# Four GEMM results in flight in PSUM in place of two, each in one bank

## The chip, the cores and the metric

The kernel runs on one core of one Trainium2 chip. The metric is the device time of one execution in microseconds. Three runs of the kernel before took 2454.41, 2458.18 and 2463.07 us (median 2458.18).

## The reference, cut to what matters

The input is x of [1, 256, 1024] in fp32, and everything is computed in fp32. One `first_block` is followed by two layers of `second_block`. Cut down to its products and what stands between them:

```
first_block:  mod = silu(c) @ w_mod + b_mod
              z = adaLN(x) @ w_in ; windowed attention, gated recurrence, blockwise attention
              x += gate * ((g0*p_a + g1*p_b + g2*p_c) @ w_out)
              x += gate * (silu(u_gate) * u_val) @ w_down      # u = causal conv over h @ w_up
second_block, twice:
              x += 0.5 * norm(swiglu(norm(x)))
              u = norm(x) @ w_in -> u_conv, q, k, v, u_pool, gates
              y_conv = silu(layer_norm(depthwise conv31(a*sigmoid(g)))) @ conv_pw
              y_attn = diff_attention(q, k, v) @ attn_o        # 8 heads of two score maps
              y_pool = ((windowed mean of u_pool - u_pool) @ w_grp * scale) @ pool_o
              x += norm((g0*y_conv + g1*y_attn + g2*y_pool) @ w_out)
              x += norm(cross_attention(norm(x), norm(mem)))
              x += 0.5 * norm(swiglu(norm(x)))
```

In `pool_branch` the 1024 columns of u_pool form four groups of 256. Each group gets its own moving mean over 2, 4, 8 or 16 rows, and its own 256x256 product `w_grp`.

## The kernel before, in words

Tokens: 256. Every dense product is a sequence of **units**: 512 KB of weights, which are four 128-row slices of 256 columns. A **GEMM result** (a "pair" in the code, numbered from 0 by `gemm`, L100) is two tiles of 128 x 256, accumulated over all units of its input features: 8 slices of features make two units. A GEMM in form F keeps features on the partitions (L866), in form T tokens (L869). fp32 precision comes from three matmuls per slice and tile: a high part of the weights with a high part of x, the same with the low part of x, and the low part of the weights with the high part of x. So a unit of four slices and two tiles is 24 matmuls.

Engines and queues of a unit m: SP starts the weights' transfer into one of 6 raw buffers as soon as that is free; ACT rounds them to the high part (`hi`, L1142) once the unit m-4 has left its buffer; DVE subtracts to get the low part (`lo`, L1475), three units ahead of PE; PE multiplies (`pe_unit`, L846 to L872). TensorE, DVE and ACT each run one instruction list in one common order of steps, which `plan()` writes out before the program is built. `spread` (L147) lays short pieces of other work behind the units: softmaxes of the attention, the taps of the depthwise convolution (L1925), windows of the pool branch. An engine that waits holds up everything behind it in its own list.

The results of GEMMs lie in `gemm_ps` (L638), four banks of PSUM, as [2 results][2 tiles][512 columns]. A tile of 256 columns fills half of a bank, so each of the two tiles of a result has a bank of its own. The other four banks (`misc_ps`) take scores, turned tiles and statistics. Before the first matmul of result p, PE waits until result p-2 has been read out (L852). Each tile's first matmul has the start flag and its last one the stop flag (L863, L864). A result is read by one or two engines (an evacuation, queued on the reader's list behind the `hi` or `lo` of the unit just before it): for the query features `vec_scaled` on DVE (L1666), for the pool inputs and values `vec_v2` on DVE (L1673, one instruction per tile), for the pool products first ACT (`act_evac_pool_w`, L1444, one per tile: the high part) and then DVE (`vec_pool_w`, L1943, one per tile: the rest).

The stretch that matters below lies in each layer of the second block, in `queries_pool` (about L455 to L485). Its steps are: pool inputs 2 and 3 (columns 512 to 1023), query features 1, window 3, pool inputs 0 and 1, window 2, query 2, window 1, query 3, window 0, and then the four pool products g = 3, 2, 1, 0. The eight heads of the differential attention are spread between them; per head PE makes scores (L1016, and L1017 for the bias), DVE takes the row maximum (L1685), ACT the exponential (L1273), DVE normalises (L1721), PE turns the result (L1034), and DVE and ACT copy it for the product with v (L1054, L1055).

Before the change the pool inputs are a GEMM of 512 columns: one result then fills its two banks, with 128x512 matmuls at L869, in four units of two slices each.

Of the kernel before, what the change touches and what calls it, by code (L numbers as in the profile page):

```python
# [17 lines left out]
F32 = mybir.dt.float32  # L18
# [5 lines left out]
P = 128  # L24
T = 256
# [15 lines left out]
RAW = 6  # L41
SPLIT = 4
AHEAD = SPLIT - 1
CONV_PARTS = 10
CONV_TAPS = (CONV_K - 1) // CONV_PARTS
NEG = -1e30
# [39 lines left out]
def plan(stop=None):  # L86
# [348 lines left out]
    def mixer(l):  # L435
# [18 lines left out]
        def queries_pool():  # L454

            after = readers.get("G")

            def inputs(j):
                z2(l, "pool", j, "evac_v2", form="T", cols=2 * COLS, dst="pt", c0=j * COLS)

            def query(j):
                z2(l, "q", j, "evac_scaled", dst="q", ft=2 * j, by=HD ** -0.5)

            def window(g):
                add("window", l=l, g=g, gen=key + "p", after=after, s=new_stat())

            inputs(2)
            query(1)
            window(3)
            inputs(0)  # L470
            window(2)
            query(2)
            window(1)
            query(3)
            window(0)
            for g in (3, 2, 1, 0):
                gemm("pool_w", 0, 2, ("G", key + "p"), "evac_pool_w", ft0=2 * g, l=l, g=g)
            merge(0, 8, "pool_o", "q", True)
# [97 lines left out]
def build(nc, a, out, scratch, marks, final, stop=None):  # L576
# [55 lines left out]
    MGS = {"b1": SQ[:], "m": o_m["pu"][:]}  # L632
    last_x = max([k["v"] for kind, k in steps if kind == "residual"], default=0)
    n_pairs = 1 + max([k["id"] for kind, k in steps if kind.startswith("evac")], default=-1)
    last_pairs = [p for p in (n_pairs - 2, n_pairs - 1) if p >= 0]


    GP = ctx.enter_context(nc.psum_tensor("gemm_ps", [P, 2, 2, 512], F32))  # L638
    PB = ctx.enter_context(nc.psum_tensor("misc_ps", [P, 4, 512], F32))
    GPF = GP[:].rearrange("p a b c -> p (a b c)")  # L640
    PBF = PB[:].rearrange("p a b -> p (a b)")
# [55 lines left out]
        return ap.unsqueeze(1).to_broadcast([P, n, T])  # L697

    def slot(pid):
        return GP[:, pid % 2, :, 0:T]  # L700

    def unit_of(buf, i, u):

# [135 lines left out]
    def _(pe):  # L839
# [6 lines left out]
        def pe_unit(u):  # L846
            xh, xl = xbuf(*u["x"])
            m = u["m"] % SPLIT
            pe.wait_ge(sems["weights_rest"], at("rest", u["m"]))
            if u["first"]:  # L850
                if u["pair"] >= 2:
                    pe.wait_ge(*done(("evac", u["pair"] - 2)))  # L852
                else:
                    pe.wait_ge(sems["vec_setup"], at("x", 0, 3))
            ps = GP[:, u["pair"] % 2, :, :]
            tiles = u["cols"] // P if u["form"] == "F" else TT
            for kt in range(u["nkt"]):
                for c in range(tiles):
                    f = u["ft0"] + u["kt0"] + kt
                    if c == 0:  # L860
                        pe.wait_ge(*done(("split", *u["x"], f)))
                    for n, (w, x) in enumerate(((WH, xh), (WH, xl), (WL, xh))):
                        start = u["first"] and kt == 0 and n == 0  # L863
                        stop_ = u["last"] and kt == u["nkt"] - 1 and n == 2  # L864
                        if u["form"] == "F":
                            mm = pe.matmul(ps[:, c, 0:T], w[:, m, kt, c * P:(c + 1) * P], x[:, f, :],  # L866
                                           start=start, stop=stop_)
                        else:
                            mm = pe.matmul(ps[:, c, 0:u["cols"]], x[:, f, c * P:(c + 1) * P],  # L869
                                           unit_of(w, m, u)[:, kt, :], start=start, stop=stop_)  # L870
            mm.then_inc(sems["gemm_done"], 1)
            up("gemm_done", ("unit", u["n"]))  # L872
# [260 lines left out]
    def _(act):  # L1133
# [125 lines left out]

        def act_evac_v1(k):  # L1260
            act.wait_ge(sems["gemm_done"], at("unit", k["last_unit"]))
            act.copy(BUF[k["dst"]][:, :, k["c0"]:k["c0"] + k["cols"]], GP[:, k["id"] % 2, :, 0:k["cols"]]).then_inc(sems["act_drain"], 1)
            up("act_drain", ("evac", k["id"]))
            mark(("tm", k["dst"], 0), "act_drain")

# [203 lines left out]
    def _(dve):  # L1469
# [200 lines left out]
        def vec_v2(k):  # L1670
            dve.wait_ge(sems["gemm_done"], at("unit", k["last_unit"]))
            for t in range(TT):
                dve.tensor_scalar(BUF[k["dst"]][:, t, k["c0"]:k["c0"] + k["cols"]], GP[:, k["id"] % 2, t, 0:k["cols"]], RT[:, t:t + 1], None, ALU.mult).then_inc(sems["vec_drain"], 1)  # L1673
                up("vec_drain", ("evac", k["id"]))
            mark(("tm", k["dst"], k["l"]), "vec_drain")
            for c in range(k["c0"], k["c0"] + k["cols"], COLS):
                mark(("tm", k["dst"], k["l"], c), "vec_drain")
# [259 lines left out]
        def vec_pool_w(k):  # L1937
            l, g = k["l"], k["g"]
            dve.wait_ge(sems["gemm_done"], at("unit", k["last_unit"]))
            for i in range(2):  # L1940
                f = 2 * g + i
                dve.wait_ge(sems["act_split"], at("split_hi", "G", f"l{l}mq", f))
                dve.scalar_tensor_tensor(out=o_m["gl2"][:, f, :], in0=slot(k["id"])[:, i, :], scalar=col(f"pscale{l}", f), in1=o_m["gh2"][:, f, :], op0=ALU.mult, op1=ALU.subtract).then_inc(sems["vec_split"], 1)  # L1943
                up("vec_split", ("split", "G", f"l{l}mq", f))
            mark(("evac", k["id"]), "vec_split")
# [171 lines left out]
```

## Time and profile before

| | |
|---|---|
| three runs | 2454.41, 2458.18, 2463.07 us |
| profiled execution | 2459.62 us, span 2457.8 us |
| granted TensorE clock, mean | 0.967 of full speed |
| TensorE (PE) | 2329.1 us busy, 95%, 17913 matmuls |
| weight loads (PEld) | 2225.7 us, 91% |
| VectorE (DVE) | 1697.4 us, 69% |
| ScalarE (ACT) | 1201.9 us, 49% |
| GpSimd (POOL) | 87.8 us, 4% |
| DMA | 397 MB read, 162 GB/s over the span |
| chain that ended last | PE 77%, DVE 15%, ACT 5%, issue 3% |

How to read it: an engine that is busy for 95% of the span is nearly always the one that the others wait for, so what a change can win is to be looked for in the stretches in which PE stands still, and in those in which its clock is granted at half speed. "issue" as a releaser means that the profile shows nothing that ended the wait; a wait for a semaphore that another engine raised can also end up under it. A row of the timeline gives start, busy time, engine and line, tiles (out<-in), and in brackets the idle time before it and what ended it. Matmuls overlap, so the distance between two starts is the cost of one, not its own length.

### The profile page before, as it was taken

The page shows a single profiled execution, that of the slowest core. Times are in us where ns is not written, and L with a number is a line of the kernel's source. Part 1 is how long each engine was busy: PE and PEld are TensorE (multiplying, and loading weights), DVE is VectorE, ACT ScalarE, POOL GpSimd, SP SyncE. Part 2 cuts the span into 40 slices and gives each one's busy share as a digit, 9 for nine tenths or more (in the row PEclk, how much of TensorE's full clock was granted, in tenths as well). Part 3 has the DMA queues.
Part 4 walks back from the last instruction along what each step waited for, and adds up shares of the span by engine and source line. Part 5 has one row for each costly group of instructions (what it writes and reads, how often), then busy time and mean ns, then how long its engine had stood idle before and what let it go on. Part 6 is the DMA issues. An engine that isn't in the chain of part 4 may idle for free.

```text
span 2457.8 us, 43525 instructions
## 1 busy us (share of the span) xinstructions
PE 2329.1 (95%) x17913; PEld 2225.7 (91%) x17913; DVE 1697.4 (69%) x2655; ACT 1201.9 (49%) x1803; POOL 87.8 (4%) x78
## 2 busy tenths in 40 slices
PE   6998898999999999999999999999999999999997
PEld 5977898999999987889898999999997889898997
DVE  6656887986664897787555664664897787555653
ACT  2565446764444434555535444444434555535443
POOL 1000000110110000000000110110000000000110
PEclk7998999999999999999999999999999999999998
DMA  8634575667656563346444655656553346444662
GB/s 241 189 103 145 161 251 160 200 188 225 182 176 190 172 179 95 112 129 189 145 139 137 181 182 159 182 176 188 173 180 95 112 130 188 146 139 136 183 184 81
DMA packets 397941, 400.89 MB, mean 163 GB/s; under 512 B 18006, under 2 KB 391112, under 8 KB 397745
## 3 DMA queue, kind: packets, MB, share of 16 engines
q1 hardware_dynamic: 395361, 389.27, 52.1%
q0 software_dynamic: 2384, 8.85, 1.1%
q8 instruction: 143, 2.34, 0.4%
q14 instruction: 53, 0.43, 0.1%
HBM read 396.98 MB, written 1.09 MB: 162 GB/s over the span
## 4 chain that ended last, share of the span: by engine, by line
PE 77%; DVE 15%; ACT 5%; issue 3%; DMA 1%; DVEq 0%; ACTq 0%; POOL 0%; POOLq 0%
PE gemm_ps L866 62%; DVE weights_lo L1475 4%; PE gemm_ps L869 4%; DVE y L1925 3%; PE misc_ps L1017 2%; PE misc_ps L1016 2%; PE misc_ps L951 2%; PE misc_ps L969 1%; DVE mod_partial L1572 1%; ACT weights_hi L1142 1%; ACT e L1273 1%; DVE y L1625 1%; PE misc_ps L1049 1%; PE misc_ps L1034 1%; PE misc_ps L1013 1%
## 5 line engine op out<-in xcount | busy, mean ns | idle before, releaser
L1475 DVE TENSOR_TENSOR weights_lo<-raw_weights,weights_hi 128x1024 fp32r<-128x1024 f32 x704 | 836.5, 1198 | 448.3 <-ACT weights_hi L1142 446.4
L866 PE MATMUL gemm_ps<-h_hi,weights_hi 128*128 128x256 f32 x3536 | 1008.8, 285 | 41.8 <-DVE h_lo L1611 27.6
L1142 ACT CAST weights_hi<-raw_weights 128x1024 fp32r<-128x1024 f32 x704 | 719.0, 1034 | 673.1 <-PE gemm_ps L866 609.5
L866 PE MATMUL gemm_ps<-h_lo,weights_hi 128*128 128x256 f32 x3536 | 995.5, 282 | 0.0
L866 PE MATMUL gemm_ps<-h_hi,weights_lo 128*128 128x256 f32 x3536 | 994.1, 281 | 0.0
L866 PEld LDWEIGHTS gemm_ps<-h_hi,weights_hi 128*128 128x128 f32 x3536 | 673.5, 190 | 50.4 <-issue 46.3
L866 PEld LDWEIGHTS gemm_ps<-h_lo,weights_hi 128*128 128x128 f32 x3536 | 673.1, 190 | 2.9 <-issue 2.2
L866 PEld LDWEIGHTS gemm_ps<-h_hi,weights_lo 128*128 128x128 f32 x3536 | 671.2, 190 | 0.0
L866 PE MATMUL gemm_ps<-hidh,weights_hi 128*128 128x256 f32 x880 | 248.4, 282 | 1.8 <-DVE weights_lo L1475 1.8
L866 PE MATMUL gemm_ps<-hidl,weights_hi 128*128 128x256 f32 x880 | 246.6, 280 | 0.0
L866 PE MATMUL gemm_ps<-hidh,weights_lo 128*128 128x256 f32 x880 | 246.3, 280 | 0.0
L1925 DVE SCALAR_TENSOR_TENSOR y<-zp,param_cols,y 128x256 f32<-128x256 f32 x480 | 196.6, 477 | 0.0
L866 PE MATMUL gemm_ps<-gh,weights_hi 128*128 128x256 f32 x544 | 163.8, 301 | 11.6 <-issue 9.3
L866 PEld LDWEIGHTS gemm_ps<-hidh,weights_hi 128*128 128x128 f32 x880 | 166.0, 189 | 2.2 <-DVE weights_lo L1475 2.0
L866 PEld LDWEIGHTS gemm_ps<-hidh,weights_lo 128*128 128x128 f32 x880 | 165.9, 188 | 0.0
L866 PEld LDWEIGHTS gemm_ps<-hidl,weights_hi 128*128 128x128 f32 x880 | 165.7, 188 | 0.2
L866 PE MATMUL gemm_ps<-gl,weights_hi 128*128 128x256 f32 x544 | 157.2, 289 | 0.0
L866 PE MATMUL gemm_ps<-gh,weights_lo 128*128 128x256 f32 x544 | 157.2, 289 | 0.0
L866 PEld LDWEIGHTS gemm_ps<-gh,weights_hi 128*128 128x128 f32 x544 | 107.9, 198 | 15.0 <-issue 12.8
L2043 POOL TENSOR_TENSOR hidl<-hf,hidh 128x512 fp32r<-128x512 f32 x55 | 73.4, 1335 | 1241.5 <-ACT hidh L1398 1241.5
L866 PEld LDWEIGHTS gemm_ps<-gl,weights_hi 128*128 128x128 f32 x544 | 107.8, 198 | 1.4 <-issue 1.0
L866 PEld LDWEIGHTS gemm_ps<-gh,weights_lo 128*128 128x128 f32 x544 | 107.6, 198 | 0.0
(289 smaller groups left out, 2665.9 us busy)
## 6 DMA issues: line engine op xcount, KB each, us to landing
raw_weights<-in_ffn_w_dram SPq DMA_DIRECT2D x256, 512.0 KB, 3.9
raw_weights<-in_w_in_dram SPq DMA_DIRECT2D x200, 512.0 KB, 3.7
raw_weights<-in_w_mod_dram SPq DMA_DIRECT2D x48, 512.0 KB, 4.9
raw_weights<-in_w_up_dram SPq DMA_DIRECT2D x44, 512.0 KB, 4.6
raw_weights<-in_xattn_kv_dram SPq DMA_DIRECT2D x32, 512.0 KB, 4.4
raw_weights<-in_w_out_dram SPq DMA_DIRECT2D x24, 512.0 KB, 4.5
raw_weights<-in_w_down_dram SPq DMA_DIRECT2D x20, 512.0 KB, 4.5
raw_weights<-in_w_branch_dram SPq DMA_DIRECT2D x16, 512.0 KB, 4.6
```

The costliest lines, as they stand in the source:

```text
L866: mm = pe.matmul(ps[:, c, 0:T], w[:, m, kt, c * P:(c + 1) * P], x[:, f, :], start=start, stop=stop_)
L869: mm = pe.matmul(ps[:, c, 0:u["cols"]], x[:, f, c * P:(c + 1) * P], unit_of(w, m, u)[:, kt, :], start=start, stop=stop_)
L951: mm = pe.matmul(STAT[:, 0:T], ONES[:], squares[:, f, :], start=f == 0, stop=f == NF - 1)
L969: mm = pe.matmul(STAT[:, 0:T], ONES[:], SQ[:, f, :], start=f == 0, stop=f == NF - 1)
L1013: mm = pe.matmul(ps, c["q"][0][f][:, qt * P:(qt + 1) * P], c["k"][0][f], start=f == 0, stop=f == 1)
L1016: pe.matmul(ps, c["q"][m][:, qt * P:(qt + 1) * P], c["k"][m][:, 0:nk], start=True, stop=False)
L1017: mm = pe.matmul(ps, FLIP[:], c["hank"][:, c["head"][m], T - nk:T], start=False, stop=True)
L1034: mm = pe.transpose(TURN[:, at_:at_ + P], c["E"][:, qt, m, kb * P:(kb + 1) * P], IDENT[:])
L1142: act.copy(unit_of(WH, m % SPLIT, u), unit_of(RAWB, u["raw"] % RAW, u)).then_inc(sems["weights_rounded"], 1)
L1475: dve.tensor_tensor(unit_of(WL, m % SPLIT, u), unit_of(RAWB, u["raw"] % RAW, u), unit_of(WH, m % SPLIT, u), ALU.subtract).then_inc(sems["w ...
L1925: dve.scalar_tensor_tensor(out=Y[:, f, :], in0=o_m["zp"][:, f, j:j + T], scalar=col(f"dw{l}", 8 * j + f), in1=Y[:, f, :], op0=ALU.mult, op ...
L2043: pool.tensor_tensor(l_[:, s, :], src, h[:, s, :], ALU.subtract).then_inc(sems["hidden_rest"], 1)
```

## The change

Three things, in the kernel's own names.

1. `gemm_ps` becomes [4 results][2 tiles][256 columns]. It is the same four banks, but both tiles of a result now lie in one bank. PE waits for result p-4 instead of p-2, and the end of the kernel waits for the last four evacuations instead of the last two.
2. The start flag stands only at the first matmul of a result's first tile, and the stop flag only at the last matmul of its last tile. One start clears the written-flags of the whole bank; the first matmul of the second tile then finds its elements unwritten and overwrites them.
3. A result can't be wider than 256 columns per tile any more. So each GEMM of 512 columns for the pool inputs is now two of 256 (`for c in (j, j + 1)`), each of two units of four slices, with two evacuations `evac_v2`, the first of which is queued two units earlier. And in `vec_pool_w` DVE waits before its first read until ACT has read both tiles, because they share a bank.

```diff
+RING = 4
...
             def inputs(j):
-                z2(l, "pool", j, "evac_v2", form="T", cols=2 * COLS, dst="pt", c0=j * COLS)
+                for c in (j, j + 1):
+                    z2(l, "pool", c, "evac_v2", form="T", dst="pt", c0=c * COLS)
...
-    last_pairs = [p for p in (n_pairs - 2, n_pairs - 1) if p >= 0]
-    GP = ctx.enter_context(nc.psum_tensor("gemm_ps", [P, 2, 2, 512], F32))
+    last_pairs = range(n_pairs - RING, n_pairs)
+    GP = ctx.enter_context(nc.psum_tensor("gemm_ps", [P, RING, 2, COLS], F32))
...
     def slot(pid):
-        return GP[:, pid % 2, :, 0:T]
+        return GP[:, pid % RING]
...
             if u["first"]:
-                if u["pair"] >= 2:
-                    pe.wait_ge(*done(("evac", u["pair"] - 2)))
+                if u["pair"] >= RING:
+                    pe.wait_ge(*done(("evac", u["pair"] - RING)))
...
-            ps = GP[:, u["pair"] % 2, :, :]
+            ps = slot(u["pair"])
...
-                        start = u["first"] and kt == 0 and n == 0
-                        stop_ = u["last"] and kt == u["nkt"] - 1 and n == 2
+                        start = u["first"] and kt == 0 and n == 0 and c == 0
+                        stop_ = u["last"] and kt == u["nkt"] - 1 and n == 2 and c == tiles - 1
...
         def vec_pool_w(k):
...
-                dve.wait_ge(sems["act_split"], at("split_hi", "G", f"l{l}mq", f))
+                dve.wait_ge(sems["act_split"], at("split_hi", "G", f"l{l}mq", 2 * g + 1))
```

The two evacuations that index `gemm_ps` themselves (L1262 and L1673) now go through `slot` too.

## Rows read from the trace of the kernel before

**Rows 1.** The page: busy time of each engine.
```profile
PE 2329.1 (95%) x17913; PEld 2225.7 (91%) x17913; DVE 1697.4 (69%) x2655; ACT 1201.9 (49%) x1803; POOL 87.8 (4%) x78
```

**Rows 2.** Waits of PE at L866 named issue: us in total, times, longest.
```profile
PE gemm_ps L866 <- issue: 10.5, 4, 4.3
```

**Rows 3.** Timeline of PE: four waits named issue.
```profile
247.73 0.36 PE L866 MATMUL gemm_ps<-h_hi,weights_hi 128*128 128x256 f32 x1 [1.24 <-issue]
...
303.17 0.55 PE L866 MATMUL gemm_ps<-gh,weights_hi 128*128 128x256 f32 x1 [0.65 <-issue]
...
974.34 0.55 PE L866 MATMUL gemm_ps<-gh,weights_hi 128*128 128x256 f32 x1 [4.32 <-issue]
...
1896.36 0.36 PE L866 MATMUL gemm_ps<-gh,weights_hi 128*128 128x256 f32 x1 [4.32 <-issue]
```

**Rows 4.** Timeline of DVE: what stands before 974.34 and after it.
```profile
973.56 0.68 DVE L1666 SCALAR_TENSOR_TENSOR q<-gemm_ps,rstd_x 128x512 f32<-128x512 f32 x1
...
982.81 1.21 DVE L1475 TENSOR_TENSOR weights_lo<-raw_weights,weights_hi 128x1024 fp32r<-128x1024 f32 x1
...
988.93 0.88 DVE L1943 SCALAR_TENSOR_TENSOR gl<-gemm_ps,param_cols,gh 128x256 fp32r<-128x256 f32 x2 [4.91 <-ACT gh L1444]
990.16 1.23 DVE L1475 TENSOR_TENSOR weights_lo<-raw_weights,weights_hi 128x1024 fp32r<-128x1024 f32 x1 [0.36 <-ACT weights_hi L1142]
...
1910.37 0.87 DVE L1943 SCALAR_TENSOR_TENSOR gl<-gemm_ps,param_cols,gh 128x256 fp32r<-128x256 f32 x2 [4.33 <-ACT gh L1444]
```

**Rows 5.** Chain that ended last, 955 to 1010 us: start, us, what.
```profile
970.02 4.32 issue
974.34 2.90 PE gemm_ps L866 x12
...
984.74 2.56 PE gemm_ps L866 x12
...
996.50 0.49 PE misc_ps L1016 x2
...
1000.75 2.83 PE gemm_ps L866 x24
```

**Rows 6.** Windows: us, busy (x count) of PE, PEld, DVE, ACT, POOL, PEclk, DMA share, GB/s.
```profile
972.10:989.00 16.90, 14.66 (x49) 11.44 (x50) 11.99 (x27) 5.23 (x11) 0.00 (x0) 0.50 0.29 93
...
1050.60:1057.20 6.60, 5.73 (x27) 5.67 (x28) 6.60 (x14) 2.81 (x4) 0.00 (x0) 0.50 0.41 116
...
801.40:804.60 3.20, 3.20 (x17) 3.20 (x16) 3.20 (x7) 2.12 (x5) 0.00 (x0) 0.50 0.95 357
...
996.50:1047.30 50.80, 50.80 (x360) 44.83 (x361) 44.05 (x90) 27.45 (x48) 0.00 (x0) 1.00 0.40 125
```

**Rows 7.** Timeline of PE: waits behind the smaller stalls, and other long waits.
```profile
273.49 1.13 PE L1054 MATMUL misc_ps<-pt,vc 128*64 128x256 f32 x4 [3.04 <-ACT pt L1283]
...
800.96 0.36 PE L866 MATMUL gemm_ps<-h_hi,weights_hi 128*128 128x256 f32 x1 [3.76 <-DVE h_lo L1611]
...
918.67 0.49 PE L1016 MATMUL misc_ps<-k,q 64*128 64x128 f32 x2 [0.42 <-ACT e L1273]
...
1051.47 0.87 PE L1034 MATMUL misc_ps<-ident,e 128*128 128x128 f32 x3 [3.87 <-DVE q L1737]
```

**Rows 8.** Timeline of DVE: evacuations of 512 and 256 columns.
```profile
953.75 1.40 DVE L1673 TENSOR_SCALAR pu<-gemm_ps,rstd_tok 128x512 f32<-128x512 f32 x2
...
882.99 0.87 DVE L1673 TENSOR_SCALAR v<-gemm_ps,rstd_tok 128x256 f32<-128x256 f32 x2
```

**Rows 9.** Timeline of PE: two starts of 512 columns.
```profile
917.62 0.39 PE L869 MATMUL gemm_ps<-weights_hi,h_lo 128*128 128x512 f32 x1
917.85 0.40 PE L869 MATMUL gemm_ps<-weights_lo,h_hi 128*128 128x512 f32 x1
```

**Rows 10.** Chain that ended last, whole span: two long series of matmuls.
```profile
410.13 120.55 PE gemm_ps L866 x1056
...
612.74 149.81 PE gemm_ps L866 x1272
```

More of the change, by code:

```diff
@@ L1261, in act_evac_v1 @@
             act.wait_ge(sems["gemm_done"], at("unit", k["last_unit"]))
-            act.copy(BUF[k["dst"]][:, :, k["c0"]:k["c0"] + k["cols"]], GP[:, k["id"] % 2, :, 0:k["cols"]]).then_inc(sems["act_drain"], 1)
+            act.copy(BUF[k["dst"]][:, :, k["c0"]:k["c0"] + k["cols"]], slot(k["id"])[:, :, 0:k["cols"]]).then_inc(sems["act_drain"], 1)
             up("act_drain", ("evac", k["id"]))
@@ L1672, in vec_v2 @@
             for t in range(TT):
-                dve.tensor_scalar(BUF[k["dst"]][:, t, k["c0"]:k["c0"] + k["cols"]], GP[:, k["id"] % 2, t, 0:k["cols"]], RT[:, t:t + 1], None, ALU.mult).then_inc(sems["vec_drain"], 1)
+                dve.tensor_scalar(BUF[k["dst"]][:, t, k["c0"]:k["c0"] + k["cols"]], slot(k["id"])[:, t, 0:k["cols"]], RT[:, t:t + 1], None, ALU.mult).then_inc(sems["vec_drain"], 1)
                 up("vec_drain", ("evac", k["id"]))
```

## The prediction

> **What bounds the kernel now.** I read the page first: PE is busy for 95% of the span, DVE for 69% and ACT for 49% [rows 1]. So a wider ring pays only where PE stands still for a result of two GEMMs ago, or where such a stall has put its clock down. The waits of PE come next. A wait for an evacuation is not named as one: at the first matmul of a result the profile writes "issue", four times at L866 with 10.5 us [rows 2]. The timeline shows what they are. At 974.34 the first matmul of the pool product g=2 has been idle for 4.32 us [rows 3]; on DVE the evacuation of query 3, two results earlier, starts at 973.56 and lasts 0.68 us [rows 4]: it ends at 974.24, and PE starts 0.1 us later. It is late because DVE has the softmax of head 3 ahead of it in its list. Layer 1 repeats this at 1896.36 (4.32). Smaller ones are at 247.73 (1.24) and 303.17 (0.65). I compared every first matmul with the end of the evacuation it needs: nine places are bound by it, with 13.3 us between neighbouring matmuls, and the other five have 0.2 to 0.7 us each (2.2 us together). All else is bound elsewhere: 0.5% of the span is at stake directly.
>
> The clock adds to that. Behind both large stalls it is granted at half, 1.2 in place of 2.4 GHz: from 972.1 to 989.0 [rows 6], and alike in layer 1. In the chain, 12 matmuls of L866 take 2.90 us there where 24 take 2.83 at full clock, and the 16 matmuls of a head's scores, which begin when these 12 end, take 984.74 - 977.24 = 7.50 us where the next head's take 1000.75 - 996.50 = 4.25 [rows 5]: 1.5 + 3.25 us, and about 1.2 for the next 12: some 6 us lost per layer.
>
> **The change part by part.** All sums are against the profiled execution, 2459.62 us (span 2457.8), which is 1.44 above the median of the runs shown.
>
> *The ring at the pool products.* With four results g=2 needs result p-4, long read. PE runs on at 970.0 instead of 974.3, at full clock: product g=2 until 971.4, scores of head 4 until 975.7, g=1 until 977.1, turn, g=0 and the product with v until about 979.8, and one unit of the first gate GEMM until 982.6. What is late next is DVE. From 974.2 to 984.0 it was continuously busy before, the last piece being the subtraction of 982.81 with 1.21 us [rows 4], and none of that gets earlier. So the next unit waits for its low part until 984.0 (1.4 us) and ends near 986.9. Behind that DVE was idle for 4.91 us until g=1 was ready and 0.36 for a rounding [rows 4]: both go, 5.27 us. Its row maximum of head 4, the exponentials behind it, and the scores of head 5, which PE began at 996.50 waiting for them, all come 5.27 earlier, at 991.2. In layer 1 the idle is 4.33 + 0.36 = 4.69. So of stall and slow clock 5.27 and 4.69 us are gained at this point, 10.0 in all; the rest turns into waits of PE: 1.4 us, and then from 986.9 to 991.2, 4.3 us.
>
> *The clock behind the new wait.* All waits of 3.8 us or more were accompanied by a half clock: 800.96 (3.76) by 801.4 to 804.6, 1051.47 (3.87) by 1050.6 to 1057.2, 974.34 and 1896.36 (4.32) as above [rows 3, 6, 7]; seven places behave so. The new wait of 4.3 us is of that size. So I expect half clock again, now at the scores of head 5: 3.25 us for their 16 matmuls, and 1.5 to 3.4 for the GEMM behind them until the clock is back; I take 5.5 per layer. Ends: if it is as short as at 801.4 (3.2 us), about 2.0; if it lasts as long behind the restart as at 974.34 to 989.0 (14.7 us, all in use), 7.4. The value is nearer to the upper end because the work behind the wait is the same head of scores. This loss has no cover: from 996.50 to 1047.3 PE has no idle time at all (50.80 of 50.80 us busy [rows 6]), and DVE, which PE next waits for at 1051.47, waits for PE in that stretch too. Sum of both: -10.0 + 2 x 5.5 = +1.0.
>
> *The other stalls.* At 247.73 the 1.3 us are given back: PE waits 3.04 us at 273.49 for ACT, which waits for a DVE that is busy throughout [rows 7]. The ones at 891.77 and 1073.9 end alike in waits for DVE (918.67, 1080.99), that of 274.98 in one for DVE at 287.56. At 303.17 (0.65) DVE is ahead, so it is gained: -0.7.
>
> *The pool inputs in 256 columns.* Each result of 128x512 read in 1.40 us by two instructions becomes two reads of 0.87 (the row is that of v, the same form [rows 8]). In the sum +0.34 us of DVE per result; but the first of the two is now queued two units earlier, and for inputs 2 and 3 that is before the row maximum of head 0, which leads by the exponentials to the scores of head 1 at 918.67, where PE waits already (0.42) [rows 7]. So its whole 0.87 us is paid in each layer: +1.7. The later half has no waiter near. Matmuls: one of 512 columns for two of 256; two of 512 start 0.23 us apart [rows 9], two of 256 take 2 x 117.8 ns [rows 10], which over the 192 matmuls of 512 columns in both layers is 0 to 1 us; I take 0.1. The transfers of these units have rows of 1 KB for 2 KB; they have six buffers ahead and 30 to 40% of the DMA time in use: nothing, and if their cover went, part of a microsecond each.
>
> *DVE waiting for both of ACT's reads.* The Trainium skill (PSUM — Partial Sum Buffer, "PSUM bank collisions raise a hardware error") has it that two engines must never touch one bank of the same partitions together; so with shared banks this order is needed, where ACT's second read could overlap DVE's first before. No row shows such a collision. By the rows, ACT is ahead: at most one ACT read of a tile is added before each of eight DVE reads of one; two of these take DVE 0.88 us [rows 4], so 0.44 each and 3.5 in all. But ACT reads a product as soon as PE is done with it (970 to 977 for g=3 to 1 in the new order), while DVE, busy with its list, comes to them from 977.7 on. I take 0; ends 0 and +3.5.
>
> *Two tiles in one bank, one start flag.* Matmuls alternate tiles, so banks alternated before every third matmul, and now they stay. No row shows an accumulation of two tiles in one bank. In this trace long series run at one of two paces: 1056 matmuls in 120.55 us (114.2 ns each), 1272 in 149.81 us (117.8) [rows 10]. Both alternate banks in the same way, so the difference is not the bank's. Ends: all 16368 are at the slow pace or as before: -3 to +4. I take 0.
>
> Sum: -0.7 + 1.0 + 1.7 + 0.1 = +2.1, 2461.7 against 2459.62; less the 1.44, **2460 us**.
>
> **The rivals.**
> *A. The same exchange of waits, but the clock stays up.* The waits of 1.4 and 4.3 us have a unit between them and full work before; the other seven had one block of idleness. Against it: 3.76 us sufficed at 800.96. Then the 11.0 go: -8.9, **2449 us**. Also in between: a short half clock (2.0 per layer) gives 2453.
> *B. The whole bubble comes back,* because DVE's list isn't late after all: the stalls (13.3) and the clock's loss behind them (6 + 5.5) go: -25, **2433 us**. For it speaks only that PE is at 95% and the stall ends with the evacuation; against it, DVE's chain from 974.2 to 984.0 and the maximum behind it, which no PSUM feeds earlier. The Trainium skill (Perfetto Trace Analysis, "Optimization Strategy") would call for this: a gap repeating on the engine that should be saturated can mean that there isn't enough PSUM for the next tile. The gap does repeat here, once per layer.
> *C. Slower: the shared bank costs pace.* The series at 114.2 ns fall to 117.8: 1056 x 3.6 ns = 3.8 us for the largest, 6.9 for all (175 us of the span run at that pace). It decides from the first GEMM on. With the clock at its long end (+3.8) this makes 2460 + 6 to 10: **2468 us**.
> *D. It doesn't do what it says:* "issue" is no wait for the evacuation. Then -0 and +1.8: 2460 too, told apart by the idle time at 974. Against it stands the 0.1 us between 974.24 and 974.34.
>
> **How the numbers follow.** Forecast (with the clock falling) 0.60, with its own range from the clock's ends, 2453 to 2464, D 0.03, A 0.17, B 0.05, C 0.15. The range 2448 to 2468 leaves out B and part of C. 0.3% or 7.4 us is about what a measurement can tell from no change, that is 2451 to 2466. Faster: A (2449 lies only just below) most of it, B, a little of the forecast: 0.23. Slower: C and a little: 0.15. Same: 0.62.
>
> **What would show it.** Right: no idle before the first matmul of product g=2 (near 970 and 1892); DVE without the 4.91 and 4.33 us before L1943; instead PE waits about 4 us at L1016 for ACT's e (head 5), and the slices with half clock come 15 to 20 us later; the scores of head 1 (918.67) begin 0.9 us later. The wait of 3.0 at 273.49 grows by 1.3. Wrong: full clock at the scores of head 5 (A), or a wait under 2 us there (B); series of L866 at another pace than 114.2 and 117.8 ns (C); the 4.32 still at 974 (D).

## The result, and the profile after

The changed kernel takes 2464.19 us (median of 20 runs, 2457.00 to 2468.67) where the kernel before takes 2456.57 (20 runs, 2451.50 to 2463.07). The ratio is 1.0031, interval 1.0023 to 1.0039: slower by 7.6 us, 5.7 to 9.6. The forecast had 2460 in a range of 2448 to 2468, so +2.1 us (0.1%) for what became +7.6 (0.3%).

The profiled executions are 3.4 us apart (2459.62 and 2463.04). I compare them stretch by stretch, because the first 400 us of a run differ by some microseconds from run to run. First the busy times, to be read against [rows 1], from the page of the changed kernel:

```profile
PE 2328.2 (95%) x18105; PEld 2232.0 (91%) x18105; DVE 1697.9 (69%) x2663; ACT 1200.9 (49%) x1803; POOL 88.0 (4%) x78
```

Nothing is to be seen there: 192 more matmuls, no more busy time. The waits of PE show the exchange (line, releaser, us in total, times, longest). Lines are shifted by 2: L868 is L866 of before.

```profile
PE misc_ps L1018 <- ACT e L1275: 11.3, 6, 4.0
...
PE gemm_ps L868 <- DVE weights_lo L1477: 5.1, 6, 1.5
```

The 10.5 us named "issue" at the first matmul of a result [rows 2] are gone from L868, and with them the 4.32 us at 974.34 and 1896.36 [rows 3]. In their place stand 11.3 us of waits for the exponentials; before it was 0.9 us in three waits. Nearly all of it is four waits, two in each layer. From PE's timeline of the changed kernel, the scores of heads 1 and 5 in layer 0 and in layer 1 (start us, us, what, idle before and its releaser):

```profile
919.37 0.49 PE L1018 MATMUL misc_ps<-k,q 64*128 64x128 f32 x2 [1.48 <-ACT e L1275]
...
994.86 0.48 PE L1018 MATMUL misc_ps<-k,q 64*128 64x128 f32 x2 [3.89 <-ACT e L1275]
...
1841.37 0.48 PE L1018 MATMUL misc_ps<-k,q 64*128 64x128 f32 x2 [1.48 <-ACT e L1275]
...
1916.93 0.49 PE L1018 MATMUL misc_ps<-k,q 64*128 64x128 f32 x2 [3.99 <-ACT e L1275]
```

The waits at 994.86 and 1916.93 were forecast (4.3). The two of 1.48 us were forecast as 0.87 us longer than the 0.42 of [rows 7]. At 919.37 that is nearly so: 1.06 longer by the idle time, 0.94 by the distance between two starts (1.76 for 0.82, the figures that the expectations below use). In layer 1 the kernel before did not wait at head 1 at all in the profile of [rows 1] (1840.69, right behind the matmul before it; 0.40 us in a second profile), so the 1.48 us at 1841.37 are all new there. What was not forecast is the clock behind them. Windows of the changed kernel (columns as in [rows 6]; the one before the DMA share is PEclk), behind each of the four waits, and the pool products:

```profile
921.20:927.90 6.70, 6.70 (x20) 4.57 (x21) 5.26 (x10) 0.00 (x0) 0.00 (x0) 0.50 0.30 86
1842.80:1849.40 6.60, 6.60 (x18) 4.24 (x19) 5.66 (x11) 0.39 (x1) 0.00 (x0) 0.50 0.25 79
996.30:1002.90 6.60, 6.60 (x18) 4.25 (x19) 6.60 (x14) 2.34 (x3) 0.00 (x0) 0.50 0.43 130
1917.90:1928.00 10.10, 10.10 (x33) 7.52 (x34) 10.10 (x22) 2.81 (x3) 0.00 (x0) 0.50 0.41 125
971.00:996.00 25.00, 19.50 (x134) 16.77 (x133) 20.93 (x48) 12.24 (x35) 0.00 (x0) 1.00 0.34 106
```

The pool products run at full clock now, 1.00 where [rows 6] have 0.50. Each of the four waits has half clock behind it.

What makes the scores of head 1 late is on DVE's timeline of the changed kernel. The row at 912.25 is the moved evacuation, the last one the row maximum, which began at 915.85 before:

```profile
911.12 1.21 DVE L1477 TENSOR_TENSOR weights_lo<-raw_weights,weights_hi 128x1024 fp32r<-128x1024 f32 x1
912.25 0.86 DVE L1675 TENSOR_SCALAR pu<-gemm_ps,rstd_tok 128x256 f32<-128x256 f32 x2
913.04 1.20 DVE L1477 TENSOR_TENSOR weights_lo<-raw_weights,weights_hi 128x1024 fp32r<-128x1024 f32 x1
914.17 2.45 DVE L1927 SCALAR_TENSOR_TENSOR y<-zp,param_cols,y 128x256 f32<-128x256 f32 x6
916.55 1.01 DVE L1687 TENSOR_REDUCE neg_max<-misc_ps 128x2 f32<-128x256 f32 x2
```

And at the pool products, where DVE waited 4.91 and 0.36 us [rows 4], its list now runs without a gap up to the maximum of head 4 (992.04), from which the scores of head 5 (994.86) follow:

```profile
985.83 0.87 DVE L1945 SCALAR_TENSOR_TENSOR gl<-gemm_ps,param_cols,gh 128x256 fp32r<-128x256 f32 x2
986.61 1.21 DVE L1477 TENSOR_TENSOR weights_lo<-raw_weights,weights_hi 128x1024 fp32r<-128x1024 f32 x1
987.75 0.86 DVE L1945 SCALAR_TENSOR_TENSOR gl<-gemm_ps,param_cols,gh 128x256 fp32r<-128x256 f32 x2
988.53 1.21 DVE L1477 TENSOR_TENSOR weights_lo<-raw_weights,weights_hi 128x1024 fp32r<-128x1024 f32 x1
989.66 2.45 DVE L1927 SCALAR_TENSOR_TENSOR y<-zp,param_cols,y 128x256 f32<-128x256 f32 x6
992.04 1.01 DVE L1687 TENSOR_REDUCE neg_max<-misc_ps 128x2 f32<-128x256 f32 x2
```

The account by stretches, from the starts of matmuls in the timelines: from the scores of head 0 to the turn of its result, and from there to the first turn behind the scores of head 5 ("turn 5"; what is turned there is the result of head 4), layer 0 and layer 1, in us.

| kernel | head 0 to turn 0 | turn 0 to "turn 5" | both layers, sum | against before |
|---|---|---|---|---|
| before | 17.17, 16.73 | 77.84, 77.24 | 188.98 | |
| before, profiled again | 17.15, 17.15 | 77.32, 77.41 | 189.03 | +0.1 |
| after | 21.23, 21.21 | 75.47, 77.07 | 194.98 | +6.0 |
| late evacuation | 20.43, 17.34 | 76.55, 75.48 | 189.80 | +0.8 |
| split alone | 20.56, 20.77 | 77.11, 77.19 | 195.63 | +6.7 |
| ring of two in the new layout | 20.77, 20.99 | 77.17, 77.16 | 196.09 | +7.1 |
| shared bank alone | 17.16, 16.64 | 77.23, 76.35 | 187.38 | -1.6 |

So 8.5 us are lost around head 1 and 2.5 are won at the pool products and head 5: +6.0 in these stretches, where the two profiled executions as a whole are 3.4 us apart and the medians 7.6. One profile per kernel says where time goes; how much of it the median keeps, only the medians tell.

### The profile page after: what moved, and what is told of

The parts are those of the page before. It is cut to its first block, busy times and chain, and to the rows that moved or that the text cites. A ratio compares the mean times of both kernels' runs of the same rounds, so it can differ in the third digit from the quotient of the medians.

```text
span 2461.2 us, 43918 instructions
## 1 busy us (share of the span) xinstructions
PE 2328.2 (95%) x18105; PEld 2232.0 (91%) x18105; DVE 1697.9 (69%) x2663; ACT 1200.9 (49%) x1803; POOL 88.0 (4%) x78
## 4 chain that ended last, share of the span: by engine, by line
PE 71%; DVE 19%; ACT 5%; issue 4%; DMA 1%; DVEq 0%; ACTq 0%; POOL 0%; POOLq 0%
PE gemm_ps L868 59%; DVE weights_lo L1477 6%; DVE y L1927 4%; PE gemm_ps L871 2%; PE misc_ps L1019 2%; PE misc_ps L1018 2%; PE misc_ps L953 1%; PE misc_ps L971 1%; DVE mod_partial L1574 1%; ACT weights_hi L1144 1%; ACT e L1275 1%; DVE y L1627 1%; PE misc_ps L1051 1%; DVE neg_max L1687 1%; DVE h_lo L1613 1%
## 5 line engine op out<-in xcount | busy, mean ns | idle before, releaser
L868 PE MATMUL gemm_ps<-h_hi,weights_hi 128*128 128x256 f32 x3536 | 1013.1, 287 | 42.6 <-DVE h_lo L1613 28.3
L868 PE MATMUL gemm_ps<-h_lo,weights_hi 128*128 128x256 f32 x3536 | 998.9, 283 | 0.0
L868 PE MATMUL gemm_ps<-h_hi,weights_lo 128*128 128x256 f32 x3536 | 997.2, 282 | 0.0
L868 PEld LDWEIGHTS gemm_ps<-h_hi,weights_hi 128*128 128x128 f32 x3536 | 675.9, 191 | 52.8 <-issue 45.6
L868 PEld LDWEIGHTS gemm_ps<-h_lo,weights_hi 128*128 128x128 f32 x3536 | 675.3, 191 | 3.5 <-issue 2.7
L868 PEld LDWEIGHTS gemm_ps<-h_hi,weights_lo 128*128 128x128 f32 x3536 | 673.3, 190 | 0.0
L868 PE MATMUL gemm_ps<-hidh,weights_hi 128*128 128x256 f32 x880 | 247.8, 282 | 1.5 <-DVE weights_lo L1477 1.5
L868 PE MATMUL gemm_ps<-hidl,weights_hi 128*128 128x256 f32 x880 | 245.9, 279 | 0.0
L868 PE MATMUL gemm_ps<-hidh,weights_lo 128*128 128x256 f32 x880 | 245.7, 279 | 0.0
L868 PEld LDWEIGHTS gemm_ps<-hidh,weights_hi 128*128 128x128 f32 x880 | 165.3, 188 | 1.9 <-DVE weights_lo L1477 1.7
L868 PEld LDWEIGHTS gemm_ps<-hidl,weights_hi 128*128 128x128 f32 x880 | 165.0, 187 | 0.2
L868 PEld LDWEIGHTS gemm_ps<-hidh,weights_lo 128*128 128x128 f32 x880 | 165.0, 188 | 0.0
L868 PE MATMUL gemm_ps<-gh,weights_hi 128*128 128x256 f32 x544 | 160.7, 295 | 2.5 <-DVE gl L1613 1.4
L868 PE MATMUL gemm_ps<-gl,weights_hi 128*128 128x256 f32 x544 | 154.4, 284 | 0.0
L868 PE MATMUL gemm_ps<-gh,weights_lo 128*128 128x256 f32 x544 | 154.2, 283 | 0.0
L868 PEld LDWEIGHTS gemm_ps<-gh,weights_hi 128*128 128x128 f32 x544 | 105.3, 193 | 5.3 <-issue 3.2
L868 PEld LDWEIGHTS gemm_ps<-gl,weights_hi 128*128 128x128 f32 x544 | 105.0, 193 | 1.4 <-issue 1.0
L868 PEld LDWEIGHTS gemm_ps<-gh,weights_lo 128*128 128x128 f32 x544 | 104.8, 193 | 0.0
```

## The experiments

The theory after the two profiles was that the early evacuation made the loss (theory E). The rival was pace: two tiles in one bank slow the long series of matmuls (theory P), for which the profile speaks. Chain of the changed kernel, the series of [rows 10]:

```profile
407.35 125.08 PE gemm_ps L868 x1056
612.66 149.81 PE gemm_ps L868 x1272
```

The first took 120.55 before, the second is the same.

**Late evacuation** (everything of the change but the early evacuation):

```diff
-                for c in (j, j + 1):
-                    z2(l, "pool", c, "evac_v2", form="T", dst="pt", c0=c * COLS)
+                got = collect(lambda: [z2(l, "pool", c, "evac_v2", form="T", dst="pt", c0=c * COLS) for c in (j, j + 1)])
+                S.extend([s for s in got if s[0] != "evac_v2"] + [s for s in got if s[0] == "evac_v2"])
```

> The changed kernel with one thing undone: the evacuations of both halves of a pool input stand behind the second half's last unit, where the 512-column evacuation stood before; nothing of DVE's is queued earlier. Theory E (the early evacuation): in the changed kernel it made PE wait 1.76 us in place of 0.82 for the scores of head 1 (near 919), the clock fell there to half for 6.8 us, and 4.0 us were lost in layer 0 and about as much in layer 1. Then this kernel shows full clock between 905 and 930, the scores of head 1 near 918.5, and is 6 to 8 us faster than the changed kernel: 2453 to 2457 where before has 2456.6. Theory P (pace: two tiles in one bank slow the long series of matmuls from 114.2 to 117.8 ns): the loss stays, 2461 to 2464 here. If both hold, 2457 to 2460.

Measured: 2459.26 us against 2457.64, ratio 1.0006 (0.9995 to 1.0016). That is 6 us better than the change's 1.0031, the intervals don't overlap, and the loss against before can't be told from none. The size is that of theory E with a bit left over: 2453 to 2457 was expected for E alone, 2457 to 2460 if E and P both held, so that the time by itself did not rule out P. And half of one expectation failed: the clock did fall in layer 0. From PE's timeline of this kernel, the scores of head 1 in layer 0 and in layer 1, and the windows behind them:

```profile
924.09 0.49 PE L1018 MATMUL misc_ps<-k,q 64*128 64x128 f32 x2 [0.73 <-ACT e L1275]
...
1846.51 0.48 PE L1018 MATMUL misc_ps<-k,q 64*128 64x128 f32 x2 [0.72 <-ACT e L1275]
```

```profile
926.90:933.60 6.70, 6.70 (x26) 5.69 (x26) 5.06 (x11) 0.00 (x0) 0.00 (x0) 0.50 0.31 90
1845.00:1851.80 6.80, 6.08 (x34) 4.35 (x34) 5.24 (x14) 3.33 (x10) 0.00 (x0) 1.00 0.22 67
```

The same work behind the same wait had half clock once and full clock once: 20.43 us against 17.34 from head 0 to its turn. Taking the profiles of all kernels that keep this order of steps together, the wait at head 1 was between nothing and 0.42 us eight times (the two profiles of before and the two of the shared bank alone), each time with full clock behind it; 0.72 and 0.73 here, once full and once half; and 0.86 to 1.48 us six times (split alone, ring of two in the new layout, after), each time with half clock. So at this place the kernel before stood on the good side of an edge, and 0.9 us more of DVE ahead of the row maximum could cost 4. It is an edge of this place only: at head 6, further below, waits of 1.5 us had full clock behind them in one kernel and half clock in another.

**Split alone** (the kernel before, with the pool inputs as two GEMMs each: the `for c in (j, j + 1)` of the change, nothing else).

> The kernel before (two results, a bank for each tile) with the pool inputs alone as two GEMMs of 256 columns, the first evacuation queued early as in the changed kernel. Theory E: half clock near 921 in layer 0 and in layer 1, 4 us each, and the idle time of 4.3 us at the pool products stays: +7 to +9 us, about 2464.5. Theory P: nothing but the matmuls' 0.5 us, 2457.

Measured: 2462.97 against 2457.64, ratio 1.0022 (1.0012 to 1.0031), +5.3 us where theory E had +7 to +9 and theory P nothing. The waits at head 1 are 0.86 and 1.06 us. This one part accounts for most of the change's loss, with two results in flight and a bank for each tile. Its waits of PE (columns as above) and the windows at head 1, pool products and head 1 of layer 1:

```profile
PE gemm_ps L867 <- issue: 10.5, 5, 4.3
```

```profile
917.90:924.60 6.70, 6.70 (x26) 5.51 (x25) 4.36 (x10) 0.00 (x0) 0.00 (x0) 0.50 0.36 93
972.60:986.00 13.40, 12.32 (x38) 9.09 (x39) 10.77 (x23) 3.05 (x5) 0.00 (x0) 0.50 0.36 111
1842.90:1849.60 6.70, 6.70 (x25) 5.35 (x24) 4.45 (x10) 0.00 (x0) 0.00 (x0) 0.50 0.38 123
```

Old idle time and new half clock stand side by side.

**Shared bank alone** (the kernel before, two results, 512-column pool inputs; narrow results with both tiles in one bank, one start flag, DVE behind both reads of ACT):

```diff
-        return GP[:, pid % 2, :, 0:T]
+        return GP[:, pid % 2].rearrange("p b (h c) -> p b h c", h=2)[:, 0]
...
-                        start = u["first"] and kt == 0 and n == 0
+                        start = u["first"] and kt == 0 and n == 0 and (wide or c == 0)
```

> The kernel before with two results in flight, but each result of 256 columns has both tiles in one bank, one start flag and one stop flag for both, and DVE's read of a pool product behind both of ACT's; the pool inputs stay at 512 columns in two banks. Only what sharing the bank costs by itself. Theory E: no difference, 2455.5 to 2458. Theory P: +4 to +7 us, 2460 to 2464, and the series of 1056 matmuls from 410 on takes 117.8 ns per matmul in place of 114.2.

Measured: 2457.64 against 2457.64, ratio 1.0000 (0.9990 to 1.0009). Sharing costs nothing that can be measured; over 2.2 us is excluded. That holds for DVE's longer wait too. Theory P falls as an explanation of the 7.6 us. Yet the series of 1056 matmuls was slow in this profile, as theory P had it. Two more profiles were to tell whether the pace belongs to the kernel or to the run.

**The kernel before, again** (no edit).

> The kernel before once more, for its profile: is the pace of a series of matmuls a property of the kernel or of the run? Theory P (sharing the bank sets the pace in the first feed-forward): the series of 1056 matmuls takes 120.55 us again, as in the two profiles of kernels with a bank for each tile. Rival R (chance): 124.4 us or more is as likely.

Measured: 2457.63 us. The chain of this execution:

```profile
407.50 126.16 PE gemm_ps L866 x1056
```

About one microsecond of this is the clock, which was at half from 408.1 to 411.5 in this execution (the series of the changed kernel, 125.08, had full clock); the rest is the slow pace.

**The shared bank, again** (no edit against the one above).

> The kernel before with both tiles of a result in one bank, once more, for its profile. Theory P: the series of 1056 matmuls takes 125 to 126 us again, as in the four profiles of kernels with a shared bank. Rival R (chance): 120.55 us is possible here too.

Measured: 2455.18 us, and its series takes 125.07. The slow pace occurs without a shared bank, so 120.55 is no property of the kernel before. Nor does sharing rule it out: one of the kernels with a shared bank further below (all spread by matmuls) has in its chain

```profile
415.06 120.55 PE gemm_ps L869 x1056
```

So both paces occur in both layouts. Over all profiles the fast one was seen in three of four executions with a bank for each tile and in one of ten with a shared bank. Whether sharing makes it rarer stays open; the interval of the shared bank alone leaves at most 2.2 us for it and for everything else that sharing does. (In the two stretches of the table that kernel was 1.6 us shorter than before, which its median doesn't show.)

**Ring of two in the new layout** (the change, but PE waits for the result two GEMMs ago):

```diff
-                if u["pair"] >= RING:
-                    pe.wait_ge(*done(("evac", u["pair"] - RING)))
+                if u["pair"] >= 2:
+                    pe.wait_ge(*done(("evac", u["pair"] - 2)))
```

> The changed kernel, whose PE waits for the result two GEMMs ago, as before, in place of four: layout, flags and pool inputs are those of the change, the deeper ring is not used. Gives what the depth is worth. Theory E: as the kernel with the split alone, +7 to +9 us against before, so the depth itself is worth 0 to 2 us and the idle time of 4.3 us is back at the pool products. Theory P: 4 to 7 us above the kernel with the split alone. Rival: the depth is worth the whole bubble, then this one is over 15 us slower than the changed kernel.

Measured: 2463.82 against 2457.64, ratio 1.0025 (1.0013 to 1.0036), +6.2 us for an expected +7 to +9, and 0.9 us above the split alone. The change itself is at 1.0031: the depth, taken by itself in this kernel, is worth nothing that can be measured. The idle time of 4.3 us is back (10.9 us named "issue" in its waits, longest 4.3), and in the table the stretch behind turn 0 is 1.8 us longer than after. Both rivals (the pace, and a bubble that comes back in full) fall.

**Ring of four, convolution behind.** If the late row maxima are what eats the gain, they should be brought forward. In the kernel before and in the changed one a piece of the depthwise convolution (2.4 us of DVE) stands right behind a unit and so ahead of the softmax and evacuations of that unit. Here it stands behind them:

```diff
+            if step[0] == "unit":
+                out += held_back
+                held_back = []
             out.append(step)
...
-                    out += slots[put]
+                    (held_back if behind else out).extend(slots[put])
```

> The changed kernel with the pieces of the depthwise convolution (2.4 us of DVE each) queued behind the other steps of their unit in place of ahead of them, so that the row maximum and the evacuations come 2.4 us earlier where a piece stood before them. Theory E (what cost the change its gain are waits of PE for the exponentials at the scores of heads 1 and 5, and the half clock behind each): the wait at head 1 (1.76 us) goes, no half clock there, 4 us less in each layer; the wait at head 5 (4.17 us) shrinks to under 2.5 us, 2 to 6 us less in each layer. Together 2444 to 2453, faster than both kernels. Rival: the waits are set by something else (ACT, or PE itself), then 2461 to 2467.

Measured: 2454.10 against 2457.20, ratio 0.9989 (0.9980 to 0.9998). It is faster than before by 0.1%, and by some 10 us than the change: the best time here, yet 1 us outside of what was expected (2444 to 2453). Head 1 starts 0.21 us behind the matmul before it, with no wait in the profile, and the window behind it is at full clock. The wait for the exponentials has moved to head 4 (2.59 us, with half clock) and to head 6 (1.51 us, with full clock), in both layers alike. From the timeline and windows of this kernel, heads 4, 5 and 6:

```profile
976.87 0.48 PE L1021 MATMUL misc_ps<-k,q 64*128 64x128 f32 x2 [2.59 <-ACT e L1278]
...
993.90 0.49 PE L1021 MATMUL misc_ps<-k,q 64*128 64x128 f32 x2 [0.21 <-ACT e L1278]
...
1012.81 0.48 PE L1021 MATMUL misc_ps<-k,q 64*128 64x128 f32 x2 [1.51 <-ACT e L1278]
```

```profile
920.00:935.00 15.00, 15.00 (x106) 13.19 (x105) 11.66 (x26) 6.69 (x22) 0.00 (x0) 1.00 0.38 121
979.10:985.80 6.70, 6.70 (x23) 5.09 (x23) 6.70 (x15) 2.33 (x4) 0.00 (x0) 0.50 0.25 78
1014.00:1020.80 6.80, 6.80 (x46) 5.58 (x45) 6.80 (x14) 3.90 (x7) 0.00 (x0) 1.00 0.26 80
```

**Ring of two, convolution behind** (the same edit on the kernel before).

> The kernel before with the same move of the convolution's pieces, ring of two, 512-column pool inputs. Tells whether the deeper ring is worth anything once the softmax is not late. Theory E: the evacuation of query 3 is still behind the softmax of head 3, but that has no piece of convolution ahead of it any more, so the idle time of 4.3 us at the pool products shrinks to about 2 us; 2447 to 2454, within 3 us of the changed kernel with the same move. Rival (the ring is what frees PE): this one stays at 2455 to 2458 and the changed kernel with the move is 5 us or more below it.

Measured: 2463.07 against 2457.20, ratio 1.0027 (1.0018 to 1.0036). Here my expectation was wrong and its rival nearly right: this order makes the ring of two 5.9 us slower, and the ring of four is 9 us below it. The idle time did not shrink to 2 us, it grew. The pool product g=2 in its PE timeline:

```profile
972.36 0.55 PE L869 MATMUL gemm_ps<-gh,weights_hi 128*128 128x256 f32 x1 [6.70 <-issue]
```

and DVE before it:

```profile
971.25 0.41 DVE L1740 COPY q<-misc_ps 128x256 f32<-128x256 f32 x1
971.58 0.68 DVE L1669 SCALAR_TENSOR_TENSOR q<-gemm_ps,rstd_x 128x512 f32<-128x512 f32 x1
```

PE comes to g=2 earlier, while the evacuation of query 3 still stands behind the softmax of head 3, which waits for PE's scores and ACT: it ends at 972.26, PE starts at 972.36. The idle time is 6.70 in place of 4.32 (6.71 in layer 1).

But that is not where this kernel loses against before. From turn 0 to the scores of head 5 its two layers take 72.61 and 67.70 us, where before has 70.92 and 70.33: 0.9 us less together. From there to the first turn behind the scores of head 6 they take 28.91 and 28.81 for 24.14 and 24.23, 9.4 us more. Two thirds of that is the clock: the scores of head 6 wait 1.50 us for the exponentials, in both layers, and have half clock behind them, where the ring of four has the same wait and full clock. From the timeline and windows of this kernel:

```profile
1012.98 0.49 PE L1019 MATMUL misc_ps<-k,q 64*128 64x128 f32 x2 [1.50 <-ACT e L1276]
...
1014.20:1021.00 6.80, 6.80 (x19) 4.41 (x19) 6.80 (x14) 3.32 (x5) 0.00 (x0) 0.50 0.26 80
1939.20:1946.00 6.80, 6.80 (x24) 5.29 (x24) 6.80 (x12) 2.28 (x3) 0.00 (x0) 0.50 0.34 100
```

So of the difference between the two rings in this order (9 us in the medians, 8.7 in the profiled executions) the profiles put 10.2 us between turn 0 and the scores of head 5, where the idle time is, and 6.2 us into the clock at head 6; the rest, -7.7, is spread over the program, nearly all of it in the first 900 us, where the long series of matmuls alone took 120.54 us in this profile and 127.41 in the other. Why the clock fell at head 6 here and not there stays open.

**Ring of three, convolution behind** (RING = 3, the tensor unchanged).

> The kernel with the convolution's pieces behind and a ring of three results in place of four (PE waits for the result three GEMMs ago, three banks used). By the trace of the kernel with four, pool product g=1 starts at 982.2 and would need the evacuation of query 3, which ends at 979.5: a third result is enough. Theory E: 2453 to 2456, as with four. Rival (depth itself pays): between 2454 and the 2463 of the ring of two, 2457 or more.

Measured: 2456.69 against 2458.60, ratio 0.9990 (0.9978 to 1.0002). As with four (0.9989), and its interval is clear of that of the ring of two (1.0018 to 1.0036): a third result is enough here. By the time alone it lies between what the theory (up to 2456) and the rival (from 2457) had; before was at 2458.60 beside it and at 2457.20 beside the ring of four.

**Convolution behind, late evacuation** (both edits above).

> The kernel with ring of four and the convolution's pieces behind (2454.1), and the pool inputs' evacuations both behind the second half, as in the kernel with the late evacuation. Theory E: the early evacuation costs only where it stands before a row maximum that PE waits for; with the pieces behind, PE no longer waits at head 1 (0.21 us between the matmuls), so it costs nothing any more: 2452.5 to 2456. Rival (the early evacuation costs by itself): 2446 to 2450.

Measured: 2456.33 against 2458.60, ratio 0.9991 (0.9983 to 1.0000). That is the 0.9989 of the early evacuation in this order, within what can be measured: the early evacuation costs nothing once no row maximum that PE waits for stands behind it. In the profile of this kernel the scores of head 6 waited 1.82 us and had half clock behind them in both layers; the median does not show it.

**Convolution behind, attention spread by matmuls** (units count by their slices where the attention's steps are spread):

```diff
+        weight = lambda k: 1 if behind else k["nkt"]
-        n = sum(kind == "unit" for kind, _ in main)
+        n = sum(weight(k) for kind, k in main if kind == "unit")
```

> The kernel with ring of four and the convolution's pieces behind (2454.1), and the attention's steps spread over the units by their number of matmuls: the four pool products are half units and count half, so the scores of heads 4 to 7 have more of PE's work between them. Theory E: the wait of 2.87 us at the scores of head 4 and the half clock behind it shrink or go, 2 to 5 us less in each layer: 2445 to 2451. Rival: DVE is the bound in this stretch (its waits just move to the next low part of the weights), then 2452 to 2456.

**Late evacuation, all spread by matmuls** (the same weight for the attention's steps and the convolution's pieces).

> The changed kernel with the late evacuation, and both the attention's steps and the convolution's pieces spread by the number of matmuls of a unit, the pieces still ahead of the softmax. Theory E: at the pool products there are half as many pieces of convolution and more of PE's work before the scores of head 5, so the wait of 4.17 us there and its half clock shrink: 2449 to 2455, where the kernel with the late evacuation alone has 2459.3. Rival (only the order of piece and softmax counts): 2457 to 2461.

Measured: 2478.43 against 2458.60 (ratio 1.0074, 1.0061 to 1.0087) and 2473.81 (1.0060, 1.0047 to 1.0073). Both are clear misses, worse than both the theory and the rival had it. The timeline of the first shows one reason:

```profile
907.74 0.76 PE L1022 MATMUL misc_ps<-k,q 64*128 64x128 f32 x2 [2.87 <-DVE q L1672]
```

Counting the half units less moves all heads, so that the scores of head 0 come one unit behind the evacuation of their own query features: PE waits for it, and the clock is at half behind that, as the window from 907.4 on shows:

```profile
907.40:917.40 10.00, 9.66 (x27) 6.67 (x28) 5.86 (x11) 1.04 (x5) 0.00 (x0) 0.50 0.53 157
```

The same profile has waits of 2.98 us ahead of the scores of head 5 in both layers, with half clock behind them. These two kernels changed more than the spacing that they were to test; that the spacing at head 5 matters was not shown by them. How the rest of the 15 to 20 us comes about I did not settle.

## Why the prediction came out as it did

**What bounds the kernel, and what "issue" is: right.** With four results the waits named "issue" left L868, and with the wait put back to two they came back (10.9 us). Rival D falls.

**The ring at the pool products: right to within 0.3 us.** From turn 0 to the scores of head 5 the two layers took 70.92 and 70.32 us before and 65.46 and 65.55 after: -5.5 and -4.8, for a forecast of -5.27 and -4.69. The new waits are 3.9 and 4.0 us where 4.3 was forecast, and the one for the low part is 1.30 and 1.21 us for a forecast of 1.4.

**The clock behind the new wait: the mechanism was right, the size too large.** From the scores of head 5 to the next turn 6.92 us became 10.02 and 11.53: +3.1 and +4.6, together 7.7, where I had 2 x 5.5 = 11.0. Rival A had none of it. This step came out 3.3 us better than forecast; with the one above it is -2.5 us for +1.0.

**The other stalls: right in kind.** That at 247.73 was given back; the wait of 3.04 us at 273.49 became 3.83, where 1.3 us more was forecast. At 303.17 the gain seems larger than the 0.7: that stretch lost its 3.4 us of half clock too, and was 2.0 us shorter. But the second profile of the kernel before has full clock there as well, with the same idle time, and against it the changed kernel is 0.6 us shorter. So the 0.7 was right, and the other 1.4 us are the run's.

```profile
303.00:306.40 3.40, 3.23 (x15) 3.26 (x16) 3.26 (x7) 1.91 (x3) 0.00 (x0) 0.50 0.11 18
303.00:306.40 3.40, 3.40 (x31) 3.40 (x30) 3.26 (x7) 1.05 (x1) 0.00 (x0) 1.00 0.52 167
```

(Windows, columns as above: the first is of the kernel before, the second of its second profile.)

**The pool inputs in 256 columns: this step failed,** as the term that was mis-sized. I had "its whole 0.87 us is paid in each layer: +1.7". The delay was right in layer 0 (the row maximum 0.70 later, PE at its wait 0.24 earlier, the wait longer by 0.94); in layer 1 it was 1.4 us, because there PE had not waited before. But behind it the clock fell at the scores of head 1, which I had considered at the long waits only: 21.23 - 17.17 and 21.21 - 16.73 us, +8.5 in all, of which the clock is 3.1 in each layer. The split alone shows it (+5.3 us in the median, +7.4 from head 0 to turn 0), the late evacuation takes 6 of the 7.6 us back, and with the convolution behind neither wait nor half clock is there. My price for the clock came from waits of 3.8 us and more; I read from them that a short wait is safe. The trace of the kernel before speaks against it, in a row that the prediction does not use: a wait of 1.79 us with half clock behind it. From its timeline and windows:

```profile
540.61 0.39 PE L866 MATMUL gemm_ps<-hidh,weights_hi 128*128 128x256 f32 x1 [1.79 <-DVE weights_lo L1475]
...
541.90:545.30 3.40, 3.40 (x19) 3.40 (x18) 3.26 (x6) 0.16 (x1) 0.00 (x0) 0.50 0.89 277
```

**DVE behind ACT's reads, and two tiles in one bank: right, nothing** (ratio 1.0000 for both together). The Trainium skill (PSUM — Partial Sum Buffer, "PSUM bank collisions raise a hardware error") makes this order necessary; no run here shows a collision, since all of them keep it, and the runs show that it is free where ACT is ahead.

**Rivals.** C had the sign and the time 4 us too high (2468), but by another mechanism, which the shared bank alone excludes. B, the bubble that comes back in full, is what the rule of the Trainium skill on consistent bubbles (Perfetto Trace Analysis, "Optimization Strategy") would lead to: the bubble was indeed one of PSUM, and more PSUM removed it, but most of the time went to the next late thing. Only where that was moved too did the depth pay, 9 us in the medians between the rings of two and four with the convolution behind, in part through the clock at head 6.

**The number: in the range, with luck.** By measured terms the sum is +8.5 - 2.5 in the two stretches and -2.0 at 303: +4.0, against 3.4 between the two profiled executions and 7.6 (5.7 to 9.6) between the medians. The term of the pool inputs was 6.8 us too small, the pair of ring and clock 3.5 us too large, and the run gave 1.4 us at 303: errors that partly cancel, in a range of 20 us. I gave "slower" a chance of 0.15, and slower is what the medians show. The rest of 2 to 6 us between the medians is not located. The pace of the long series (4.5 us in the profiled pair) is a candidate, but it varies from run to run in both layouts.

## What to carry to other kernels

Before a buffer is made deeper, ask which instruction list the stall comes from: here the evacuation was late because DVE's list was, and a deeper ring only carried PE on to the next thing on the same list. Then look at what the deeper ring forces elsewhere (here narrower results, and so an instruction that moves ahead of a row maximum), for a small delay in front of a short stretch can cost several times itself through the clock (here 0.9 us became 4.1 in layer 0). And when the clock is priced from a trace, read the short waits in it too, not only the long ones. Depth and order belong together: the new order alone cost 5.9 us, the depth alone cost or won nothing measurable, both together won 3.

## What the runs showed of the hardware that was not expected

A wait of 1.48 us ahead of the scores of head 1 had half clock behind it in both layers, one of 0.73 us in one layer and one of 0.72 not in the other. The waits of 3.9 and 4.0 us had at least 6.6 and 10.1 us of half clock behind them. Ahead of the scores of head 6, with the convolution behind, waits of 1.50 us (ring of two) had half clock behind them and waits of 1.51 us (ring of four) full clock, each in both layers. And in one and the same kernel, before, the same wait of 1.93 us had full clock behind it in one execution and half clock in the other:

```profile
1164.87 0.36 PE L866 MATMUL gemm_ps<-h_hi,weights_hi 128*128 128x256 f32 x1 [1.93 <-DVE h_lo L1611]
1165.90:1169.30 3.40, 3.40 (x31) 3.40 (x30) 2.50 (x6) 1.75 (x2) 0.70 (x1) 1.00 0.12 32
...
1164.49 0.36 PE L866 MATMUL gemm_ps<-h_hi,weights_hi 128*128 128x256 f32 x1 [1.93 <-DVE h_lo L1611]
1165.90:1169.30 3.40, 3.40 (x19) 3.40 (x18) 1.92 (x4) 0.72 (x2) 0.70 (x1) 0.50 0.24 28
```

So neither the length of a wait nor the kernel decides what the clock does behind a wait of 0.7 to 2 us; what else does, no run here shows.

The kernel before ran its series of 1056 matmuls in 120.55 us in one profiled execution and in 126.16 in another, 3.4 us of the latter at half clock.
